# Experts' weights loaded whole, expert by expert, and a third of the last projections moved ahead of the attention scores

## The reference

```
logits = jnp.dot(h, w_router) + b_router
top_logit, top_idx = lax.top_k(logits, TOP_K)
gates = jax.nn.softmax(top_logit, axis=-1)
...
g = jnp.minimum(xb @ w_gate[e] + b_gate[e], SWIGLU_LIMIT)
u = jnp.clip(xb @ w_up[e] + b_up[e], -SWIGLU_LIMIT, SWIGLU_LIMIT)
act = g * jax.nn.sigmoid(SWIGLU_ALPHA * g) * (u + 1)
return act @ w_down[e] + b_down[e]
```

## Time and profile before

| | us |
|---|---|
| median of 3 runs | 2707.42 |
| lowest and highest | 2702.99, 2712.85 |
| the profiled execution | 2703.1 |
| its span on the core | 2701.4 |

### The profile page before, as it was taken

How to read it: one execution, slowest core, us unless ns; L and a number is a source line. 1 busy time by engine, 2 the same in 40 slices (tenths; PEclk the granted TensorE clock), 3 DMA queues, 4 the chain that set the end, 5 groups by cost and what they waited for, 6 DMA issues and landing times. The chain is left out here.

```text
span 2701.4 us, 33603 instructions
## 1 busy us (share of the span) xinstructions
PE 2512.8 (93%) x12943; PEld 1534.0 (57%) x12944; DVE 1056.0 (39%) x2206; ACT 370.9 (14%) x747; POOL 43.0 (2%) x64
## 2 busy tenths in 40 slices
PE   6998999999999799997999989998999999988998
PEld 2543333333333233335878857867876887756786
DVE  1243122221121122224382258756996433244433
ACT  2122111111111111111122110011002000132001
POOL 0000000000000000000000000000100000000000
PEclk8998999999999899998989999999999999999999
DMA  8604999999997899998433368844997543141442
GB/s 333 264 9 165 427 429 429 428 429 428 428 429 335 341 428 429 428 410 313 167 125 133 148 222 331 289 162 155 379 380 273 195 166 109 69 156 36 144 165 100
DMA packets 188020, 728.26 MB, mean 270 GB/s; under 512 B 9758, under 2 KB 103292, under 8 KB 159156
## 3 DMA queue, kind: packets, MB, share of 16 engines
q1 hardware_dynamic: 168324, 651.29, 61.6%
q0 software_dynamic: 19632, 76.09, 7.1%
HBM read 726.30 MB, written 1.05 MB: 269 GB/s over the span
## 5 line engine op out<-in xcount | busy, mean ns | idle before, releaser
L1498 PE MATMUL bank<-experts_raw,experts_xs 128*64 128x512 f32 x2112 | 475.9, 600 | 15.9 <-DMA experts_raw<-in_w_up 13.6
L1498 PEld LDWEIGHTS bank<-experts_raw,experts_xs 128*64 128x64 f32 x2112 | 147.9, 138 | 334.5 <-issue 295.1
L2384 PE MATMUL bank<-big,ffn_actT 128*128 128x512 f32 x704 | 309.1, 592 | 0.0
L1498 PE MATMUL bank<-experts_raw,tiled_act_s 128*64 128x512 f32 x1056 | 240.4, 601 | 51.7 <-DMA experts_raw<-in_w_down 50.5
L1797 PE MATMUL bank<-hT,ring 128*128 128x256 f32 x1024 | 225.0, 383 | 4.1 <-DMA ring<-in_w_in 2.9
L1797 PEld LDWEIGHTS bank<-hT,ring 128*128 128x128 f32 x1024 | 196.7, 192 | 32.9 <-issue 5.8
L2384 PEld LDWEIGHTS bank<-big,ffn_actT 128*128 128x128 f32 x704 | 130.6, 190 | 148.3 <-issue 148.3
L1632 DVE COPY tiled_spread<-bank 128x256 f32<-128x256 f32 x33 | 14.0, 425 | 441.2 <-PE bank L1534 441.2
L1498 PEld LDWEIGHTS bank<-experts_raw,tiled_act_s 128*64 128x64 f32 x1056 | 71.1, 137 | 199.1 <-issue 122.4
L2259 PEld LDWEIGHTS bank<-hT,big 128*128 128x128 f32 x1408 | 164.4, 193 | 18.5 <-issue 18.5
L2259 PE MATMUL bank<-hT,big 128*128 128x128 f32 x1408 | 165.5, 276 | 0.3 <-DVE hT L454 0.3
(11 more groups left out here) (478 smaller groups left out, 2629.3 us busy)
## 6 DMA issues: line engine op xcount, KB each, us to landing
experts_raw<-in_w_gate SPq DMA_DIRECT2D x64, 2048.0 KB, 23.7
experts_raw<-in_w_up SPq DMA_DIRECT2D x64, 2048.0 KB, 25.1
experts_raw<-in_w_down SPq DMA_DIRECT2D x64, 2048.0 KB, 25.5
big<-in_ffn_w_gu SPq DMA_DIRECT2D x88, 1024.0 KB, 9.4
ring<-in_mod_w POOLq DMA_DIRECT2D x30, 2048.0 KB, 10.7
big<-in_ffn_w_down SPq DMA_DIRECT2D x44, 1024.0 KB, 5.0
ring<-in_w_in SPq DMA_DIRECT2D x16, 2048.0 KB, 8.6
mla_wm<-in_w_mod SPq DMA_DIRECT2D x24, 1024.0 KB, 6.7
```

The costliest lines, as they stand in the source:

```text
L1498: last = nc.tensor.matmul(bank[b][h * HALF:(h + 1) * HALF, :], stationary(kt), raw[p][:, k, h * C:(h + 1) * C], start=kt == 0, stop=kt == ...
L2384: last = nc.tensor.matmul(bank[b][:], actT[:, s, f, t * P:(t + 1) * P], wd[:, s, f, n * 512:(n + 1) * 512], start=start and f == 0, stop=s ...
```

## The change

Three things are moved; no instruction that computes is added or taken away.

1. SP loads gate, up and down of expert e together, before anything of expert e + 1. Before, down of expert e - 1 came behind gate and up of expert e.
2. PE makes the down product of item e - 1 between the gate and the up product of item e, and gathers behind it. The spreading now stands behind up, directly ahead of the turns that wait for DVE's copy of it. ACT takes its results in the same order.
3. In the second block one of the three MERGE rounds is made ahead of the heads' scores, and ACT takes it ahead of the exponentials. One round stays in front of the second sum, one behind it.

```
-            load(1, 0)
-            load(1, 1)
-            with sp.Fori(2, E) as e:
-                load(e, 0)
-                load(e, 1)
-                load(e - 1, 2)
-            load(E - 1, 2)
+            with sp.Fori(1, E) as e:
+                for m in range(3):
+                    load(e, m)
...
             with pe.Fori(1, items) as e:
-                gate_up(e)
+                expert = gate(e)
+                down(e - 1)
+                gather(e + 1)
                 turn(e + 1, g_rows, g_copied, G, g_turned)
+                up(e, expert)
                 spreading(e - 1, x_copied, e + 1)
-                down(e - 1)
                 after(pe, spread_ready, e)
...
             with act.Fori(1, items) as e:
-                take_gu(e)
+                take_g(e)
                 take_y(e - 1)
+                take_u(e)
                 take_x(e + 1)
...
+            project(1)
             for h in range(H2):
                 b, o = 5 + h % 3, 64 * (h % 2)
...
-            project(2)
+            project(1)
             pe.wait_ge(*S["squared"].next(pe))
...
+            take(MERGE, 1, ACT.Sigmoid)
             for h in range(H2):
                 act.wait_ge(*S["neg_top"].next(act))
...
-            take(MERGE, 1, ACT.Sigmoid)
```

More of the change, by code:

```diff
@@ L1500, in product, with gate @@
                     last.then_inc(used[p], 1)
-            def gate_up(e):
+            def gate(e):
                 after(pe, xs_ready, e)
@@ L1506, in gate_up, with up @@
                 product(expert, 0, G, lambda kt: tiles(xs)[:, kt % 4, kt // 4, :])
-                gather(e + 1)
+                return expert
+            def up(e, expert):
                 after(pe, u_taken, e)
@@ L1547, in scatter @@
                             op.then_inc(*core.filled[2 * t + h].up())
-            gate_up(0)
+            first = gate(0)
+            gather(1)
+            up(0, first)
             turn(1, g_rows, g_copied, G, g_turned)
@@ L1588, in take_y, with take_g, take_u @@
                 run(ys[:], bank[Y][:], ACT.Copy).then_inc(y_copied, 1)
-            def take_gu(e):
+            def take_g(e):
                 after(act, used[PARTS - 1], e + 1)
                 run(g_rows[:], bank[G][:], ACT.Copy).then_inc(g_copied, 1)
+            def take_u(e):
                 take_rows(e + 1)
@@ L1597, in take_gu @@
                 run(sig[:], gate[:], ACT.Sigmoid, scale=SWISH).then_inc(sig_ready, 1)
-            take_gu(0)
+            take_g(0)
+            take_u(0)
             take_x(1)
             with act.Fori(1, items) as e:
-                take_gu(e)
+                take_g(e)
                 take_y(e - 1)
+                take_u(e)
                 take_x(e + 1)
```

## The result

| | before | after |
|---|---|---|
| median of 8 runs, us | 2707.8 | 2724.7 |
| lowest and highest, us | 2701.9, 2712.9 | 2717.3, 2731.9 |
| the profiled execution, us | 2703.1 | 2726.4 |
| its span, us | 2701.4 | 2724.7 |

The change makes the kernel slower: ratio 1.007, 95% interval 1.005 to 1.009, which is +13.5 to +24.4 us, +16.9 us by the medians. The forecast was +28, 2736. The time lies in its range of 2701 to 2750, and at the upper edge of rival (b), 2716 to 2725, where it meets the likeliest case, 2725 to 2747.

What follows compares the result with a forecast made beforehand. Weight transfers were taken to bound the experts, PE the second block. The terms, 28 - 1.9 + 3.4 + 6.4 - 7.6 = +28.3 us on 2703.1, gave 2731.4, plus 4.3 to the median: some 2736, range 2701 to 2750.

Steps and rivals of the forecast that it cites:

- rival (b): Experts: a late issue costs half as much, 0.3 to 0.6 us per expert, 2716 to 2725 us; chance 0.12.
- the likeliest case: Experts: a late issue costs 0.6 to 1.4 us per expert, 2725 to 2747 us; chance 0.50.
- What bounds the kernel: Weight transfers bound the experts, 29.35 us per expert against 26.6 of PE per item; PE bounds the second block.
- Term 1: Down buffer in every expert: freed late, so its load lands late, 1.0 us in about 28 experts, +28 us.
- rival (a): Experts: the queue takes the late issue for nothing, the other terms remain, 2708 us; chance 0.22.
- Term 2: PE's item in the experts: grows to 27.3 us by waiting for DVE's copy, still covered by the transfers, nothing.
- Term 3: Expert with two items: the 15 us wait goes, but transfers pause three times instead of twice, -1.9 us.
- Term 4: Start of the experts: down of expert 1 is issued late, behind gate of item 1, +3.4 us.
- Term 5: End of the experts: last gate and up come 9.8 us later, with a chain behind them, +6.4 us.
- Term 6: Second block: a round in front hides DVE's norms, 18.0 us instead of 25.6 between rounds, -7.6 us.
- (c): Experts: late issue costs 1.4 to 1.8 us each, or PE's item outgrows the transfers, 2745 to 2760 us; chance 0.08.
- (d): Faster by over 0.3%: free late issues plus a cheaper end or a higher second-block clock, 2690 to 2699 us; chance 0.08.

Runs made afterwards that it cites:

- loads alone: The kernel before with only SP's load order changed, PE's order and the second block as before: 3045.1 us in a single run.
- gathering first: The changed kernel with the gathering ahead of the down product instead of behind it: 2779.0 us, ratio 1.0272.
- behind six steps: The changed kernel with down's first half made behind six of gate's eight steps, its second half behind the last two: 2710.6 us, ratio 1.0013.
- halves in turn: The changed kernel with PE making first half of gate, first half of down, then the second halves: 2704.7 us, ratio 0.9991.
- the two other kernels that keep the experts of before: The kernel before with only the second block's round moved, 2700.0 us; that with the heads' scores laid between quarters of the rounds, 2691.5 us.
- the pieces: The kernel before with the second block's round moved and the heads' scores laid between quarters of two rounds: 2691.5 us, ratio 0.9943.

## Why the prediction was right, and where not

**What bounds the kernel** holds: the transfers in the experts, by the slices and by PE's waits, which now are all for gate.

**Term 1** was right in its mechanism and too large: 0.69 us per expert instead of 1.0, in 29 experts instead of 28 (2 to 31 less the repeated one), 20 us instead of 28. The step that was mis-sized is the time of the issue. I had it at 7.6 us after gate's second half, it is at 7.13: there is no time for reading the expert's number ahead of down (507.64 to 511.12 is 3.48), and from the start of the product to the issue it is 3.65, not 3.84. With 8.2 for the landing that gives 0.66. The cut from 1.25 to 1.0, because the rows came from empty queues, had no ground: the landing of down's first half on a queue with 2.6 us of work in front is the same 8.2 as on one with 0.8 or none. It brought the forecast nearer to the result by luck, since it made up for part of the late issue time.

The first halves of down in the steady experts, medians of each trace (the work ahead is the time from the issue to the landing of the half in front):

| us of work ahead of the issue | issue to landing | late |
|---|---|---|
| none (loads alone) | 8.2 | 11.6 |
| 0.8 (gathering first) | 8.2 | 2.5 |
| 2.6 (the change) | 8.2 | 0.7 |
| 4.3 (behind six steps) | 9.2 | 0 |
| 7.3 (halves in turn) | 12.2 | 0 |

The bound of "more than 3 us of work" is borne out by these halves: by 8.2 - 4.9 = 3.3 us a late issue begins to cost, and 4.3 cost nothing. With the halves in turn, six second halves of down that were issued with 3.84 us ahead also landed in their turn, 8.7 us after their issue. But 8.2 us isn't what every late half takes. The last half of before was 1.1 late with 3.4 us ahead, and the same half 1.8 and 1.3 late in the two other kernels that keep the experts of before, with 3.5 and 3.7 ahead. Three halves elsewhere, one each in the runs with the halves in turn, behind six steps and with the loads alone, had 2.5 to 2.9 us ahead and took 9.5 to 10.2 us, 2.0 to 2.4 late. No run isolated the cause, so the 3.3 us is the least lead that is needed and not one that always suffices.

The 6.8 us that the sum of the Trainium skill (DMA: Bandwidth & Descriptors, Anatomy of one DMA) leads to would have made the term nothing and rival (a) the result. The traces do not agree for SyncE's loads: down's first halves took 8.2 in the median in each of the three kernels whose issue was late.

**Term 2**: PE's item is 27.88 us, not 27.3, and it is covered in the steady part, as said: the steady items have a wait for gate of about 1.1 and one of 1.24 us.

**Term 3**: 26.4 us for the extra item instead of 28.0 before, forecast 26.2 instead of 28.1. The three pauses of the transfers came as worked out, 11.5, 6.2 and 8.8 us for 11.5, 6.5 and 8.2.

**Term 4**: the half issued at 303.98 landed 2.2 us late, forecast 3.4; the half in front of it landed 1.2 us after that issue, and I had put it at the same moment.

**Term 5**: the last product began 25.7 us after the last gate's landing, forecast 25.9, so 9.8 + 25.7 - 29.3 = +6.2. The wait for DVE that was to show it, about 6 us, is one of 1.41: between the spreading at 1244.40 and the product at 1250.28 are the 5.9 us, but PE fills most of them with two turns, a scatter and a spreading.

**Term 6**: -7.6 forecast, -7.5 and -7.7 in the two traces, and -8.4 to -2.4 by the runs of that part alone. It came closest of the terms; all of it was read from one stretch whose pace, DVE's, the change doesn't touch.

**The sum** with the sizes as measured: 0.69 x 29 = 20.0, and 20.0 - 1.6 + 2.2 + 6.2 - 7.6 = +19.2, within the interval of +13.5 to +24.4. Terms 1, 3, 4 and 5 make +26.8, and the stage of the experts shows +26.9; that the two agree to 0.1 us is luck, since the 29 late landings summed one by one are 20.5 and not 20.0. The rivals: (a) is refuted by the late landings of three kernels; (b) holds the measured time at its edge but not the size per expert, which is 0.69 where its own was 0.3 to 0.6; (c) and (d) did not come.

## What to carry to other kernels

Where one queue feeds a stage without a pause, ask of each buffer when it comes free, not whether it is free when its data is wanted: an issue needs, in front of it, as much queued work as its time to landing on an idle queue exceeds one transfer's share of the rate, here 8.2 - 4.9 = 3.3 us at least, and each microsecond below that was paid once per turn of the loop. Some halves with 2.5 to 4.5 us in front were later than that sum gives, by 0.3 to 2.0 us, so a lead just above it is no guarantee. An engine with little idle time that paces itself on another one (here PE on DVE, 18 us) is to be given its own long work in pieces between the short steps, not in one block ahead of them: the block gave 7.6 us, the pieces 7.9 more. Reordering that takes away the largest single wait (15 us here) is worth little if the wait only shows that buffers come free late: the pauses in the transfers came back in three smaller parts.

## What the runs showed of the hardware

The time from issue to landing of down's first half, 2 MB, was 8.2 us in the median with 2.6 us, 0.8 us or no work in front of it (8.0 to 8.9 from half to half), which I had not expected to be so constant: an overlap with the tail of the half ahead did not shorten it. Three other halves with 2.5 to 2.9 us in front took 9.5 to 10.2.

With the halves in turn PE waits for gate once per item, up to 1.98 us. In six items, mostly every fifth, the first product behind the wait ran at a granted clock of 0.67 on average, between the two levels of 1.2 and 2.4 GHz:

```profile
497.90:501.30 3.40, 3.40 (x16) 1.19 (x18) 1.48 (x9) 0.00 (x0) 0.00 (x0) 1.00 1.02 434
527.30:532.40 5.10, 5.10 (x16) 1.55 (x18) 1.48 (x9) 0.00 (x0) 0.00 (x0) 0.67 1.03 437
```

The same product takes 3.4 us in the one and 5.1 in the other, though PE had waited 1.97 us ahead of the one and 1.96 ahead of the other: the length of the wait just before doesn't tell them apart. In the changed kernel, whose steady items wait about 1.1 and 1.24 us with 3.65 us of work between, the granted clock stayed at 1.00 from 330 to 860 us and from 950 to 1220. With the new order of the loads alone, where PE waits 11.55 us, the first half of gate takes 5.96 us, at 0.61. What decides whether the clock falls was not tried by itself.
